# Second block's first joint on unscaled rows, and one output row moved between two heads' scores

## The reference, cut to what matters

```
# first block, behind its two layers
x = x * rsqrt(mean(x*x) + eps) * final_g
# second block, first site
h = x * rsqrt(mean(x*x) + eps) * g[0]
x = x + 0.5 * rmsnorm(swiglu(h, w_gate, w_up, w_down), g[1])
```

## Time and profile before

| | |
|---|---|
| median of 3 runs | 1495.39 us (1495.19 to 1502.93) |
| profiled execution, whole | 1496.1 us |
| profiled execution, its span (first to last instruction) | 1494.2 us, mean granted TensorE clock 0.998 |
| PE busy | 1450.9 us (97%) |
| DVE busy | 986.2 us (66%) |
| ACT busy | 703.0 us (47%) |
| POOL busy | 66.2 us (4%) |
| chain that ended last | PE 87%, DVE 5%, DMA 3%, ACT 2%, issue 2% |

### The profile page before, as it was taken

How to read it: one execution, slowest core, us unless ns; L and a number is a source line. 1 busy time by engine, 2 the same in 40 slices (tenths; PEclk the granted TensorE clock), 3 DMA queues, 4 the chain that set the end, 5 groups by cost and what they waited for, 6 DMA issues and landing times.

```text
span 1494.2 us, 22138 instructions
## 1 busy us (share of the span) xinstructions
PE 1450.9 (97%) x8141; PEld 1172.4 (78%) x8141; DVE 986.2 (66%) x1631; ACT 703.0 (47%) x1212; POOL 66.2 (4%) x91
## 2 busy tenths in 40 slices
PE   5999989999999999999999999999999999999998
PEld 3778746867845888889978888878888888788887
DVE  2588335264335777777687777686777776877776
ACT  3433146132235444456566444464444756554444
POOL 0200120010101000000010000000000001000000
PEclk9999999999999999999999999999999999999999
DMA  9532175254315566555434566555564754355562
GB/s 332 194 95 74 57 233 180 85 185 144 113 35 201 169 199 205 186 183 142 156 106 149 195 198 197 167 173 180 173 201 150 212 149 143 127 164 173 192 201 86
DMA packets 197717, 242.96 MB, mean 163 GB/s; under 512 B 4464, under 2 KB 179088, under 8 KB 197520
## 3 DMA queue, kind: packets, MB, share of 16 engines
q1 hardware_dynamic: 194560, 229.43, 48.2%
q0 software_dynamic: 2512, 10.49, 2.0%
q10 hardware_dynamic: 576, 2.10, 0.4%
HBM read 240.95 MB, written 1.05 MB: 162 GB/s over the span
## 4 chain that ended last, share of the span: by engine, by line
PE 87%; DVE 5%; DMA 3%; ACT 2%; issue 2%; SPq 0%; POOL 0%; DVEq 0%; ACTq 0%; POOLq 0%
PE bank L1740 37%; PE bank L2230 20%; PE bank L2231 10%; PE bank L1859 5%; PE bank L2137 1%; DMA weight_ring<-in_w_ada 1%; PE bank L1718 1%; DMA weight_ring<-in_w_in 1%; DVE input_split L1374 1%; DMA weight_ring<-in_w_ffn_up 1%; DVE weights_low L1341 1%; PE bank L2082 1%; ACT weights_high L863 1%; PE bank L2045 1%; PE bank L2004 1%
## 5 line engine op out<-in xcount | busy, mean ns | idle before, releaser
L1341 DVE TENSOR_TENSOR weights_low<-weight_ring,weights_high 128x1024 fp32r<-128x1024 f32 x328 | 392.9, 1222 | 134.6 <-ACT weights_high L863 134.6
L2230 PE MATMUL bank<-input_split,weights_high 128*128 128x512 f32 x1344 | 479.6, 399 | 1.3 <-DVE input_split L1374 1.0
L863 ACT ACTIVATE weights_high<-weight_ring 128x1024 fp32r<-128x1024 f32 x328 | 334.8, 1049 | 107.4 <-PE bank L1740 62.3
L2231 PE MATMUL bank<-input_split,weights_low 128*128 128x256 f32 x1344 | 377.1, 281 | 0.0
L2230 PEld LDWEIGHTS bank<-input_split,weights_high 128*128 128x128 f32 x1344 | 252.5, 188 | 65.4 <-issue 1.8
L2231 PEld LDWEIGHTS bank<-input_split,weights_low 128*128 128x128 f32 x1344 | 253.8, 189 | 3.0
L1740 PE MATMUL bank<-weights_low,hidden_high 128*128 128x512 f32 x352 | 137.9, 392 | 0.0
L1740 PE MATMUL bank<-weights_high,hidden_high 128*128 128x512 f32 x352 | 137.9, 392 | 0.0
L1740 PE MATMUL bank<-weights_high,hidden_low 128*128 128x512 f32 x352 | 137.0, 389 | 0.0
L928 ACT ACTIVATE silu_gate<-gate_sum 128x256 f32<-128x256 f32 x88 | 36.8, 418 | 206.8 <-DVE gate_sum L1424 203.8
L1740 PE MATMUL bank<-input_split,weights_high 128*128 128x256 f32 x640 | 117.9, 286 | 0.8 <-DVE input_split L1374 0.7
(11 more groups left out here) (329 smaller groups left out, 2097.3 us busy)
## 6 DMA issues: line engine op xcount, KB each, us to landing
weight_ring<-in_w_ffn_gate SPq DMA_DIRECT2D x44, 1024.0 KB, 5.3
weight_ring<-in_w_ffn_up SPq DMA_DIRECT2D x44, 1024.0 KB, 5.3
weight_ring<-in_w_ffn_down SPq DMA_DIRECT2D x44, 1024.0 KB, 4.9
weight_ring<-in_w_in SPq DMA_DIRECT2D x32, 1024.0 KB, 5.3
weight_ring<-in_w_ada SPq DMA_DIRECT2D x24, 1024.0 KB, 6.8
weight_ring<-in_w_out SPq DMA_DIRECT2D x16, 1024.0 KB, 5.0
weight_ring<-in_w_in SPq DMA_DIRECT2D x24, 512.0 KB, 5.1
gain_row<-in_norm_gains POOLq DMA_DIRECT2D x6, 512.0 KB, 4.2
```

Source lines behind the costliest of these rows:

```text
L863: A(unit_in(WH, U), unit_source(U), ACT.Copy).then_inc(s_high, 1)
L1341: TTn(unit_in(WL, U), unit_source(U), unit_in(WH, U).bitcast(F32), ALU.subtract).then_inc(s_low, 1)
L2230: mm(b[:, :].rearrange("p (h n) -> p h n", h=2), unit_in(WH, U)[:, k, :], HX[:, k, :, :], start=(k == 0), stop=False, skip_group_check=True)
L2231: last = mm(b[:, 0:T], unit_in(WL, U)[:, k, :], HH[:, k, :], start=False, stop=(k == KD - 1), skip_group_check=True)
```

## The change

Three things are done together.

1. `out_row(0, 0)` stands ahead of `scores(1)`.
2. The joint works on the unscaled `X`. PE's `turned` waits for the updated halves of `X` instead of the scaled ones; the chunks are multiplied by `first_gain`, the product of the final gain and the site's gain (a new tile of 128 x 8, made once at the program's start from a vector that the host adds to `k_vec2`). The root of the final norm is multiplied in at the end: into the reciprocals ahead of `norm_diag` and, squared, into the value that stands for eps at the site's tail. `X` itself is still scaled, tile 0 ahead of the low parts of the input split, tile 1 behind them; each waits for the transposes that read it (`x_read`, `x_T`). Four squares of the scaled `X` follow on ACT behind the split. `ADDED` of this layer gains (0, 1), so DVE adds two halves and POOL two. Six `warm` products become one, and one more stands between the two tiles' transposes.
3. `low(2)` and `low(3)` move behind the input split, on both sides of the scaling of tile 1.

```diff
-ADDED = [{(0, 1), (1, 1)}, {(1, 1)}]
+ADDED = [{(0, 1), (1, 1)}, {(0, 1), (1, 1)}]
...
+            final_square(0, 0)
+            final_square(0, 1)
+            final_root(0)
+            final_square(1, 0)
...
                 for c in range(KD):
                     act.wait_ge(*at("x_T", "site", i, c if c < 4 else 4 + c % 2))
...
+                if i == 0:
+                    final_square(1, 1)
+                    final_root(1)
+                    for hf in range(2):
+                        x_square(0, 0, hf)
...
                 if L:
-                    for unit in range(EARLY):
+                    for unit in range(2):
                         low(unit)
...
+            def final_scaled(t):
                 dve.wait_ge(*at("final_root", t))
+                dve.reciprocal(stat[:, 56 + t:57 + t], stat[:, 54 + t:55 + t]).then_inc(*done("inverse", "final", t))
                 dve.wait_ge(*at("inverse", "final", t))
+                dve.wait_ge(*(at("x_T", "site", 0, 5) if t else at("x_read", 0)))
...
+            final_scaled(0)
...
+                if i == 0:
+                    low(2)
+                    final_scaled(1)
+                    low(3)
...
+                        for q in range(2):
+                            if q:
+                                dve.wait_ge(*at("x_mean", "rescaled", 0))
+                            TTn(stat[:, 10:12], stat[:, 10:12] if q else stat[:, 6:8], stat[:, 54:56], ALU.mult).then_inc(*done("x_mean", "rescaled", q))
...
+                if i == 0:
+                    TTn(stat[:, 12:14], stat[:, 12:14], stat[:, 56:58], ALU.mult).then_inc(*done("inverse", "both"))
...
                 if L:
                     out_banks()
+                    out_row(0, 0)
...
-                    if L and i == 0:
-                        out_row(0, 0)
...
-                        pe.wait_ge(*(at("x_new", i - 1, t, c // 4) if i else at("final_scaled", t, c // 4)))
+                        pe.wait_ge(*(at("x_new", i - 1, t, c // 4) if i else x_half(1, t, c // 4)))
...
-                warm(1 if i else WARM)
+                warm(1)
                 turned(0, (0, 1, 2, 3))
                 warm(1)
                 turned(0, (4, 5, 6, 7))
+                if i == 0:
+                    warm(1)
```

51 lines of the change are left out of this document (31 added, 20 removed).

## The result

The changed kernel takes **1505.81 us** (median of 20 runs, 1500.74 to 1511.41), the kernel before 1499.12 us in the 20 runs beside it: a ratio of **1.0044, interval 1.0031 to 1.0057**, so some 6.6 us slower. The three runs that the prediction had of the kernel before lay low in its spread (1495.19 to 1505.51), which is 3.7 us of the distance between 1505.81 and the forecast of 1496.8; the other 5.3 us are the change's. The outcome lies outside the range that I gave (1490.0 to 1499.5), and it would with the better base too: I had forecast +1.4, at most +4.1. It is still within the 0.5% that I gave 0.91, on the slow side.

A forecast was written before the change was run, and what follows sets the result against it. PE, busy 97% of the span, bounds the kernel. Attention -3.6, joint -4.75, norm +3.0, up piece +5.05 and clock +1.7 sum to +1.4 us: 1496.8 us against a median of 1495.39, range 1490.0 to 1499.5.

The forecast's parts named there:

- the sum of the four at 0.40 MB/us: Behind the joint: gate piece, POOL's two loads and up piece, 4.59 MB, take 11.4 us; up piece lands at 485.1.
- The output row: Attention: the row moved between the scores fills PE's idle time and removes the low clock, -3.6 us.
- The joint up to the first product: At the joint: the site's products start 8.35 us early, 4.75 of it from the joint.
- DVE's two added halves at 0.92: At the joint: each half that DVE adds to the residual takes 0.92 us.
- The norm: Behind the joint: PE idles 3.0 us for `norm_diag`, ready at 476.05, and goes on 5.35 us early.
- The loads: Behind the joint: ring and POOL share by packet turns; late up piece costs +5.05 us, `down(0)` at 487.2 against 487.51.
- My upper bound: Loads behind the joint: at 0.327 MB/us, the up piece lands at 487.1 instead of 485.1.
- The clock: Behind PE's 5.0 us wait for the up piece: low clock costs +1.7 us, between 0 and twice that.
- The gain tile of 128 x 8 at the start: nothing: Program start: one DVE operation of about 0.2 us in small waits beside the loads, costing nothing.
- the loads are in time: Rival, behind the joint: only the norm's wait is left, -5.35 or -3.6, so 1490.0 to 1491.8 us; chance 0.15.
- The base: Whole kernel: the time before the change, taken as the runs' median of 1495.39 us.
- both upper prices: Behind the joint: up piece at 487.1 and low clock twice as long, together +5.1 us; left out of the range.

The follow-up runs named there:

- the row alone: Kernel before with only the second layer's first output row moved ahead of the second head's scores; 1495.56 us against 1499.27, ratio 0.9978.
- gain in the vector tile: Changed kernel with its gain placed in a free part of the raw vectors' tile, so no other tile moves; 1504.03 us, ratio 1.0034 to the kernel before.
- 256 bytes: Changed kernel with the gain's tile made 64 columns wide, of which 8 are used; 1503.05 us against 1501.11 for the kernel before, ratio 1.0019.
- joint alone: Changed kernel with the output row put back behind the second head's scores; 1509.66 us against 1499.42 for the kernel before, ratio 1.0067.
- POOL's loads late: Changed kernel with POOL's gain row and `alibi` loads waiting until the next up piece has landed; 1500.04 us, ratio 1.0005 to the kernel before.
- the first eight experiments: The first eight follow-up kernels, by the order of the study's table after the changed kernel; ratios to the kernel before from 0.9978 to 1.0067.
- the first four experiments: By table order: the row alone, POOL's loads late, the tile alone, gain in the vector tile; ratios 0.9978, 1.0005, 1.0012, 1.0034.
- the tile alone: Kernel before with an unused 128 x 8 tile declared where the changed kernel has its gain tile, shifting later tiles 32 bytes; 1500.60 us, ratio 1.0012.

## Why the prediction was wrong, point by point

The steps that failed, in short: the up piece's landing was mis-sized ("the sum of the four at 0.40 MB/us", 11.4 us where it took 12.9), the gain tile was put at nothing (it costs about 1.5), and the clock behind the late piece costs 1.5 to 2.8 us in the traces with this joint where the sum had 1.7. Besides, the base of three runs was low by 3.7. Of these only the base would by itself have carried the forecast beyond 1499.5, to 1500.5; the miss is their sum. The points one by one:

- **The output row: right.** Predicted 3.6 us, no idle time and full clock; the trace has 3.68, and the row alone is faster by 3.7 us in the medians. In its trace only 2.35 of the 3.7 reach the fourth block, which the sum did not allow for.
- **The joint up to the first product: right but for a size.** Predicted 8.35 us early, measured 7.98. The step that was off is DVE's two added halves at 0.92: they took 1.33 and 1.26. The one of the earlier trace rows overlapped POOL's add for 0.37 us, these overlap it for 0.78 and 0.72. In all five adds of the two traces what is left without the overlap is the same: 0.92 - 0.37, 1.33 - 0.78, 1.26 - 0.72, and 1.20 - 0.65 and 1.29 - 0.74 in the first layer, 0.54 to 0.55 each time. So DVE's add stands still while POOL's runs, and the first layer of the kernel before showed it already:

```profile
294.54 1.28 POOL L603 TENSOR_TENSOR residual<-residual,scaled_out 128x512 f32<-128x512 f32 x1 [78.13 <-DVE scaled_out L1113]
295.17 1.20 DVE L1117 TENSOR_TENSOR residual<-residual,scaled_out 128x512 f32<-128x512 f32 x1
```

  The Trainium skill (SBUF — State Buffer, Who interferes with whom) states that a VectorE operation with two inputs in SBUF contends with a GpSimd one that reads SBUF; 1.33 against 0.92 agrees.
- **The norm: right.** Predicted a wait of 3.0 us and the diagonal ready at +56.84; measured 2.74 and +56.97.
- **The loads: right in kind, short in size.** The order of issue and the turns by packet came as forecast, the up piece issued at +54.5 and found at +54.7. It took 12.9 us and not 11.4, so the first down product stood 1.41 us later than before where I had it 0.3 earlier. The step was "the sum of the four at 0.40 MB/us", to the last byte. While POOL's rows ran it held (407 GB/s from 484 to 486). But by 486 only some 0.15 MB of the up piece were in, and the other 0.90 came behind `alibi` in the ring's own 1 KB packets: 0.21, 0.32, 0.28 and 0.09 MB in the four microseconds from 486 on, where 0.40 MB/us would have needed 2.3. My upper bound (487.1 instead of 485.1) held it.
- **The clock: right in this trace, too low for the runs.** 1.7 us predicted, 1.53 measured (the step from +1.41 to +2.94). The three other kernels with the same joint and the late piece have 2.05 (gain in the vector tile), 2.28 (256 bytes) and 2.83 (joint alone). In the first two the clock falls behind the norm row's wait of 2.74 too and is back before the late piece, as I had allowed for at no cost; behind that piece it stays low for 6.8 us as here, but more of it falls on work. Windows of the kernel with 256 bytes:

```profile
482.00:484.00 2.00, 2.00 (x9) 1.74 (x9) 1.76 (x3) 1.99 (x4) 0.00 (x0) 0.60 0.91 369
...
498.00:500.00 2.00, 2.00 (x7) 1.53 (x6) 1.06 (x3) 1.29 (x3) 0.00 (x0) 0.64 0.54 88
```

- **The joint and row together** thus gave +2.94 where +1.4 was forecast: in this trace the late piece's size alone.
- **"The gain tile of 128 x 8 at the start: nothing": wrong.** This is the step whose mechanism I had missed altogether. I priced its one operation and not its place. It costs about 1.5 us in the first layer, ahead of everything that I had looked at.
- **That a shift reaches the end unchanged: a step that I took without writing it.** The sum took each shift at the first down product as a shift of the end. The joints ahead of later blocks change it: +0.72 and +0.39 at the next two, -1.97 at the last (with the gain in the vector tile +1.25, +0.39 and -1.03). For leads it is worse: of 3.5 to 4.0 us in the first block 0.8 to 2.1 were left in the second. So the rival "the loads are in time", 1490.0 to 1491.8, could not have come either: the kernel that makes it true (POOL's loads late) came out level with the kernel before.
- **The base.** The time was set against a median of three runs, 1495.39; of twenty it is 1499.12.
- **The range.** It left out the case of both upper prices at once. With the tile's 1.5 us, the late piece's 1.7 and the base's 3.7 on top of 1496.8 the sum is 1503.7; 2.1 us are left to 1505.81.

What is left is in part luck of the traces. The changed kernel's profiled execution ends with a lag of 2.08 us from `scores(0)` on; the two kernels that have its joint and not its tile end with 4.49 (gain in the vector tile) and 3.45 (256 bytes). With that, the tile's 1.5 and the 0.3 outside the span the sum is 5.3 to 6.3 us, against 6.6 between the kernels.

Much of this goes by the clock. The mean granted clock of the runs is 0.9928 in the changed kernel and 0.9961 in the kernel before (64 runs of it beside the first eight experiments). Where the up piece is late it is 0.992 to 0.994 (changed kernel, gain in the vector tile, joint alone, 256 bytes), in all others with more than one run 0.995 to 0.997. The low stretch shown above is 6.8 us at half speed, 3.4 in 1500, which is 0.0023; the low stretch in the attention that the change takes away is worth 0.0011 the other way, so the two traces explain 0.0012 of the 0.0033. In 93 runs of the kernel before, 0.001 less of mean clock goes with 1.29 us more time (an estimate, a straight line through the runs of each chip). By it 4.2 us of the changed kernel's 6.6 go with the lower clock, and at equal clock it is 2.4 us slower (1.6 to 3.2, against the 35 runs beside the first four experiments). The same estimate makes the tile alone 2.2 us slower (1.4 to 3.0), clear of no difference. Where in the program the changed kernel's other low stretches fall no trace shows, since its only trace, with a mean of 0.997, has none but those shown and the one at the end.

## What to carry to other kernels

Read how a lead or a lag fares at the next joint before adding it to the time: if a supply chain (here a ring of three loads) runs at its own pace, it passes only what it gains itself, and a wait ahead of the next block swallows the rest. When a step releases loads later, list which other queue's loads get in front of them and how long their rows are: against rows of 14 KB a ring of 1 KB rows got a fourteenth of the bytes. Price a new tile by what it moves as well as by what it computes; the test is the old kernel with the tile unused. And take the base from as many runs as the result will have, and compare the mean granted clock of both before reading a difference of a few microseconds from two traces.

## What the runs showed that I had not expected

- 32 bytes more in front of the other tiles: products of 128x512 every 0.2333 us instead of 0.2312, in the first layer only; the feed-forward products kept 0.229 us in all kernels. With 64 bytes only the later of the two stretches is slower (42 products in 9.80 us instead of 9.61), with 256 neither. Which tile or which engine's access is at fault stays open.
- A DVE add of two tiles in SBUF that overlaps POOL's add takes 0.55 us and the overlap on top.
- A single wait of 1.98 us on PE was followed by a stretch at the 1.2 GHz level, one of 1.29 or 1.65 us was not, nor were the waits of 1.4 to 1.9 us at the second joint, though one of 1.98 us there was. The wait of 2.74 us at the norm row was followed by one with POOL late, but not in the changed kernel; before, 1.74 us in the attention was and 1.74 us at 1172 was not. The length of the wait alone doesn't tell it.
- How far the turns by packet go: in 4 us the ring moved 0.12 MB of 1.67, and alone, behind that, no more than 0.32 MB in a microsecond.
